# Thirty-two experts: one counted loop, or the loop written out; and where GpSimd stores y

## The reference, cut to what matters

```python
# 2048 tokens, D = 1024, 32 experts, FF = 256, two experts a token
eid, weights = route(h)                        # 4096 assignments
xb = h_pad[buf_tok].reshape(n_blocks, 128, d)  # tokens sorted by expert, padded to 128
def expert_block(xblk, e):
    return (silu(xblk @ w_gate[e]) * (xblk @ w_up[e])) @ w_down[e]
out = zeros.at[buf_tok].add(yb * buf_w[:, None])
```

## Time and profile before

| what | value |
|---|---|
| median of 3 runs | 3301.76 us (3297.97 to 3304.68) |
| the profiled execution: own time / its span | 3296.91 / 3295.3 us |
| TensorE busy | 2678.3 us, 81% of the span |
| TensorE weight load / VectorE / ScalarE / GpSimd | 64% / 55% / 50% / 16% |
| row gathers L1266 | x194, busy 199.6 us |
| stores of y L1282 | x101, busy 121.0 us, idle before 338.3 us, 322.3 of it ended by ScalarE's y |
| splits L1330 / L1372 | x256 / x256, 1047 / 1221 ns |
| HBM traffic | 167 GB/s over the span |

### The profile page before, as it was taken

One profiled execution on the slowest core, in us unless ns is written; L12 is line 12 of the kernel. 1 busy time (PEld: TensorE's weight loads), 2 busy tenths in 40 slices (PEclk: granted clock), 3 DMA queues, 4 the chain that ended last, 5 costly groups with the idle time before them and its releaser, 6 DMA issues. The chain is left out here.

```text
span 3295.3 us, 49089 instructions
## 1 busy us (share of the span) xinstructions
PE 2678.3 (81%) x12246; PEld 2124.9 (64%) x12247; DVE 1821.4 (55%) x3423; ACT 1640.8 (50%) x2254; POOL 528.3 (16%) x792
## 2 busy tenths in 40 slices
PE   4999969999699678888883999999699488888840
PEld 3777747777588556666662777777588366666630
DVE  3444434444356546455554688877466576545645
ACT  3444544454344346455553566765344365545633
POOL 0000000000001134334330000000011244333410
PEclk8999979999899789999996999999799799999975
DMA  3111121111444279778866445431544399777857
GB/s 110 34 50 45 51 64 45 45 51 41 152 135 152 73 266 323 238 248 293 273 202 221 165 164 167 165 115 58 176 132 147 134 354 319 234 233 242 280 204 280
DMA packets 358062, 550.28 MB, mean 167 GB/s; under 512 B 32097, under 2 KB 273905, under 8 KB 353905
## 3 DMA queue, kind: packets, MB, share of 16 engines
q1 hardware_dynamic: 323296, 436.20, 40.6%
q0 software_dynamic: 32400, 104.95, 8.6%
q10 hardware_dynamic: 2304, 8.39, 0.6%
HBM read 428.29 MB, written 121.18 MB: 167 GB/s over the span
## 5 line engine op out<-in xcount | busy, mean ns | idle before, releaser
L1372 DVE TENSOR_TENSOR experts_gu_lo<-experts_gu_raw,experts_gu_hi (+1 forms) x256 | 296.7, 1221 | 151.3 <-ACT experts_gu_hi L1330 151.3
L117 PE MATMUL experts_ps<-experts_gu_hi,experts_hT_hi 128*128 (+1 forms) x760 | 321.5, 423 | 48.9 <-issue 25.6
L1330 ACT ACTIVATE experts_gu_hi<-experts_gu_raw (+1 forms) x256 | 249.8, 1047 | 121.6 <-DMA experts_gu_raw<-in_moe_w_up 76.9
L119 PE MATMUL experts_ps<-experts_gu_hi,experts_hT_lo 128*128 (+1 forms) x760 | 304.3, 400 | 0.0
L118 PE MATMUL experts_ps<-experts_gu_lo,experts_hT_hi 128*128 (+1 forms) x760 | 304.0, 400 | 0.0
L117 PE MATMUL route_ps<-route_w_hi,route_src_hi 128*128 128x512 f32 x512 | 213.2, 416 | 59.6 <-DVE route_w_lo L958 59.6
L887 POOL MEMSET route_empty<- 128x512 int32 x2 | 1.1, 549 | 1439.2 <-POOLq L159 1439.2
L1266 POOL DMA_INDIRECT experts_rows<-h_rows,experts_source_now x194 | 199.6, 1029 | 171.9 <-POOL experts_source_now L1262 138.8
L1384 DVE TENSOR_TENSOR experts_hT_lo<-experts_ps,experts_hT_hi 128x512 fp32r<-128x512 f32 x194 | 133.2, 687 | 156.3 <-ACT experts_hT_hi L1308 151.8
L1423 PE MATMUL experts_ps<-ident,experts_rows 128*128 128x128 f32 x776 | 122.1, 282 | 117.0 <-DMA experts_rows<-h_rows,experts_source_now 116.6
L117 PE MATMUL gla_ps<-gla_wvg_hi,gla_hT_hi 128*128 128x512 f32 x512 | 212.7, 415 | 0.0
(11 more groups left out here) (304 smaller groups left out, 6511.2 us busy)
## 6 DMA issues: line engine op xcount, KB each, us to landing
experts_gu_raw<-in_moe_w_gate SPq DMA_DIRECT2D x64, 1024.0 KB
experts_gu_raw<-in_moe_w_up SPq DMA_DIRECT2D x64, 1024.0 KB, 12.5
experts_wd_raw<-in_moe_w_down SPq DMA_DIRECT2D x64, 1024.0 KB, 6.0
gla_w_raw<-in_gla_w_in SPq DMA_DIRECT2D x18, 1024.0 KB, 6.6
route_src<-oT_rows SPq DMA_DIRECT2D x32, 512.0 KB, 4.2
x_rows<-route_x_new SPq DMA_DIRECT2D x32, 512.0 KB, 2.9
h_rows<-route_h SPq DMA_DIRECT2D x64, 256.0 KB, 2.3
lru_y_ab<-y_rows SPq DMA_DIRECT2D x16, 1024.0 KB, 7.7
```

The lines of the kernel that those rows point to most:

```text
L117: nc.tensor.matmul(out, w_hi, x_hi, start=first, stop=False)
L119: return nc.tensor.matmul(out, w_lo, x_hi, start=False, stop=last)
L1330: nc.scalar.activation(gu_hi[:, slot(e), of_part(c)], gu_raw[:, slot(e), of_part(c)], ACT.Copy)\
L1372: nc.vector.tensor_tensor(gu_lo[:, slot(e), of_part(c)], gu_raw[:, slot(e), of_part(c)], gu_hi[:, slot(e), of_part(c)].bitcast(F32), ALU.s ...
```

## The change

**The loop over experts is written out 32 times** on ScalarE, VectorE, TensorE, GpSimd and SyncE. The route stage packs four counts into one word, in base 32 (`PACK`, `place_value`), with one multiply and one reduce in place of a scan and its two neighbours. Each engine reads eight words into registers once, before its first expert, takes a count out of a word by shift and mask, and keeps the running sum in a register. The slots of gate/up become constants, so the `stand` before those splits goes; TensorE's `down` keeps its register address.

**GpSimd's order**: in iteration g it gathers the first half for block g+1, stores the y of g-1 (not of g), then gathers the second half. The list of a block is kept one place later (`LAG` 4).

**The start of the stage**: two memsets (`wd_hi`, `wd_lo`) go from GpSimd to VectorE, and the first column of `sources` is made on its own, so that the first gather waits for that alone.

```diff
+PACK, PACK_BASE = 4, 32
...
-            step(nc.vector.tensor_tensor_scan(upto[:], k.ones_row[:], nblk[:], 0.0, ALU.mult, ALU.add))
-            step(nc.vector.tensor_tensor(upto[:], upto[:], nblk[:], ALU.subtract))
-            step.add(nc.vector.tensor_copy(k.blocks[:], nblk[:]))
-            step.add(nc.vector.tensor_copy(k.block_at[:], upto[:]))
-            step.wait()
+            by_word = nblk[:].rearrange("p (w i) -> p w i", i=PACK)
+            step(nc.vector.tensor_tensor(by_word, by_word,
+                                         k.place_value[:].unsqueeze(1).to_broadcast([P, E // PACK, PACK]),
+                                         ALU.mult))
+            step(nc.vector.tensor_reduce(packed[:], by_word, AX.X, ALU.add))
+            step(nc.vector.tensor_copy(k.blocks[:], packed[:]))
...
+        def expert_blocks(eng, each, before=None):
+
+            words = [eng.value_load(k.blocks[0:1, w:w + 1], min_val=0, max_val=PACK_BASE ** PACK - 1)
+                     for w in range(E // PACK)]
+            first = 0
+            for e in range(E):
+                n = (words[e // PACK] // PACK_BASE ** (e % PACK)) % PACK_BASE
                 if before:
-                    before(e, s)
+                    before(e, first)
                 with eng.Fori(0, n) as b:
-                    (each or each_of(n))(e, b, nc.s_assert_within(s + b, min_val=0, max_val=MAX_BLOCKS - 1))
...
+                    each(e, b, nc.s_assert_within(first + b, min_val=0, max_val=MAX_BLOCKS - 1), n)
+                first = nc.snap(first + n)
...
         def slot(e):
-            return slice(e % 2, e % 2 + 1) if isinstance(e, int) else bass.ds(e % 2, 1)
+            return slice(e % 2, e % 2 + 1)
...
-            with sp.Fori(0, E - 2) as e:
+            for e in range(E - 2):
...
+            def each(e, b, g, n):
+                last = 1 - (n - b + (SLOTS - 2)) // SLOTS
+                column = (e * SLOTS + b + 1 + last * (SLOTS - 1 - b)) % (E * SLOTS)
+                column = nc.s_assert_within(column, min_val=0, max_val=E * SLOTS - 1)
+                name_rows(0, column, g + 1)
+                gather(0, g + 1)
+                name_targets(g - 1)
+                store_y(g - 1)
+                name_rows(1, column, g + 1)
+                gather(1, g + 1)
+                keep_list(column, g + 1)
...
+            nc.vector.memset(wd_hi[:, 1].bitcast(F32), 0.0)
+            nc.vector.memset(wd_lo[:, 1].bitcast(F32), 0.0).then_inc(wd_zeroed, 1)
```

More of the change, by code:

```diff
@@ L209, in _ @@
             done.add(pool.memset(k.eps[:], EPS))
+            for i in range(PACK):
+                done.add(pool.memset(k.place_value[:, i:i + 1], float(PACK_BASE ** i)))
             done.add(pool.iota(k.token[:], [[2 * P, NT], [1, 2]], base=0, channel_multiplier=2))
@@ L1219, in load @@
             def load(e, landed, into, w):
-                if not (isinstance(e, int) and e == 0):
+                if e:
                     sp.wait_ge(landed, nth_dma(e - 1))
-                sp.dma_start(into, w[bass.ds(e, 1)].rearrange("e (k p) c -> p e k c", p=P)).then_inc(landed, DMA)
+                sp.dma_start(into, w[e:e + 1].rearrange("e (k p) c -> p e k c", p=P)).then_inc(landed, DMA)
             def load_gu(e):
@@ L1328, in split_gu @@
                 for c in range(PARTS):
-                    stand(act)
                     nc.scalar.activation(gu_hi[:, slot(e), of_part(c)], gu_raw[:, slot(e), of_part(c)], ACT.Copy)\
@@ L1347, in before, with each @@
             def before(e, first):
-                if not is_last(e):
+                if e + 1 < E:
                     split_gu(e + 1)
                 split_wd(e, first)
-            def each(e, b, g):
+            def each(e, b, g, n):
                 take_aT(g)
@@ L1445, in _ @@
             pe.wait_ge(zeroed, 1)
+            pe.wait_ge(wd_zeroed, 1)
             for b in range(2):
```

101 lines of the change are left out of this document (45 added, 56 removed).

## The result

The changed kernel takes **3214.71 us** at the median of 4 runs (3209.87 to 3217.18), against 3300.60 for the kernel before (4 runs, 3297.97 to 3304.68): a ratio of 0.9737, 95% interval 0.972 to 0.9754. That is 86 us less, where the forecast of 3178 us meant about 123. The profiled execution took 3209.87 us, with a span of 3208.1 us.

A forecast was written before the change was run, and what follows sets the result against it. TensorE's waits in both experts stages bound it: 77.6 + 74.9 us idle and 13 of clock, 165.5 at stake. Less 30 (transfers), 14 (store chain), 2.5 (aT), plus 1 (starts): 120 us gained, 3178 us for the median; range 3148 to 3238.

The forecast's parts named there:

- Reads at the turn: Two register reads with checks go from TensorE's 62 turns between experts, worth up to 49.9 us of its waits.
- The rest of the aT chain: Earlier ScalarE splits remove nearly all 31.1 us of down products' waits for aT's low part; 2.5 us charged as left.
- GpSimd's order: the first gather: Issued ahead of the store, 3.4 us into the block, it lands before its transposes; worth up to 69.9 us of row waits.
- The second gather: On GpSimd, it takes the first gather's old place in time and is due 3.4 us later, leaving 1.5 us to spare.
- The clock: Most of 13 us lost to TensorE's half clock in both experts stages returns, since row waits cause it.
- The store chain: Store, landing, y, store: charged 14 us (0 to 47). As a rival it paces every block: 3211 us, chance 0.15.
- The full stretches: In 255 us where transfers pace the experts stages, 30 us of TensorE's 40 us idle stays; bounds 10 and 40.
- More instructions: The written-out loop adds about 26 instruction pieces for TensorE and 30 for the rest; counted 0 us.
- Rows stay late: Rival: the second gather takes over the first's wait and clock dips stay; 61 us gained, 3236 us, chance 0.15.
- Late instructions: Rival: engines stand until the 56 added instruction pieces are fetched in the experts stages; 3357 us, chance 0.03.
- refetched loops: Rival: repeated inner loops straddling two instruction pieces are fetched again, 52 fetches; 3344 us, chance 0.03.
- no difference: Rival: the turn's reads and gathers lie beside transfers that bound both experts stages; chance 0.02.

The follow-up runs named there:

- e4: The changed kernel, but each engine loads the packed word again at every expert instead of eight words once before the loop: 3223.9 us.
- e1: The experts' loop written out with packed counts as in the changed kernel, but GpSimd's order and lag 3 of the kernel before: 3252.6 us.
- f1: The changed kernel, but from the third expert on each weight load brings only an eighth of its bytes: 3098.4 us.
- e6: The changed kernel with the copy of the target row numbers made by ScalarE instead of GpSimd: 3210.3 us.
- e3: The changed kernel with both gathers ahead of the preceding block's store on GpSimd: 3299.2 us.
- e2: The kernel before with GpSimd's new order alone (lag 4), keeping the loop over experts and its register loads: 3263.7 us.
- e5: The changed kernel with TensorE's transposes of the second half of the rows moved behind the down products: 3407.0 us.
- f2: The changed kernel with ScalarE's and VectorE's copies of aT moved ahead of the next expert's weight splits: 3237.3 us.

## Why the prediction was right, and where it was off

The range (3148 to 3238) holds the time, the direction was right, and both mechanisms acted. The likeliest case was 37 us too fast.

- **Reads at the turn, up to 49.9 us.** Right, and too small. All 49.9 us of idle are gone, and 60 turns gave back 0.24 us each of overlap that the idle column doesn't hold: 15 us. e4 narrows it down: a single read at each turn costs little (2.2 us of waits). Which of the second read, the loop's branches and the register addresses cost most stays open.
- **The rest of the aT chain, 2.5 us.** Wrong as told. That ScalarE's splits start at once behind its last rows is so (the splits of 1230.17 follow the rows of 1229.66 without a gap), and e1, which has only that part, is left with 4.1 us of aT_lo waits. With the new order 25.7 us are back, in few and long ones (13, up to 6.3 us, against 31 of at most 1.5). Blocks then run at TensorE's pace into the runs of one-block experts, and the weights come late, ahead of each of the 13 (2.54 us at 1244.15). f1, whose splits are the same, has none of these waits, so the transfers and not the splits are the cause. In the sum this belonged to the full stretches.
- **GpSimd's order: the first gather.** Right in the main: it is released by the transposes, and of its 69.7 us of waits 6.4 are left. It is issued 4.3 us into the block (median), not 3.4.
- **The second gather, "1.5 us to spare, a thin cover".** This is the step that failed. It took the second gather to be issued at the place in a block that the first had before, and so to keep 1.5 us. The first had been issued 9.0 us after a block's first gate/up product (median over both windows); the second is now issued at 10.4. What the same edit puts between the two gathers on GpSimd's queue (the rest of one issue, a copy, a store, a copy, and two waits of 0.9 us for its own copies) makes 5.6 us at the median, and that uses up the 1.5: a slow landing is then a wait. The step moved was costed for the store and for y, not for the gather right behind it. 40.1 us of row waits stayed, 33.6 of them the second gather's, where the sum had none outside the full stretches. e6 and e3 point to the queue, f1 shows that it takes the loaded landing with it.
- **The clock, 13 us back.** None came back. The waits left are fewer (55 against 145) but as long, up to 3 us for rows, and the lower level follows them. By the windows' means, 1% of 510 and 3% of 492 us are 20 us, where the same reckoning gave 5.6 + 10.6 = 16 before (the prediction took 13). So some 4 us more were lost than before.
- **The store chain, 14 us (bounds 0 and 47).** Named directly, TensorE waits for y 3.9 us in all. The chain acts on another path than the one priced: a y that waits for its store makes the next store late, and with it the second gather. Its share of the 40.1 us of row waits was not told apart from the queue's. Where the store is issued 2 us later (e3), it holds the down products and costs more than the rival's 47 us (84 us in all).
- **The full stretches, 30 us left (10 to 40).** f1 says that all of what is left, 71.9 us of idle but for 7, goes away when the weight loads are small. The 30 was too low, and the waits it leaves out are those of the two points above on aT and the second gather.
- **More instructions, 0.** Right: 28 and 38 more packets, no stall of TensorE. The Trainium skill's rule ("Runtime: NRT & Kernel Launch", section "Instruction fetch mechanics", a taken branch out of a window of two pages stalls) would have cost 88 us by the estimate given; the trace shows none of it. The same section names such stalls as one reason why kernels prefer full unrolling. Writing the loop out did gain 47.6 us here (e1), but the loop before had fetched next to nothing in its stage (3 packets), so the gain was not in the fetches.
- **Not foreseen.** The stages ahead of the first experts stage have the same code and yet took 5.8 us more (it begins at 1156.1 and not 1150.3 us); in every kernel with the loop written out it begins at 1152.7 to 1158.7, in e2 at 1149.2. Against the kernel before, the delay comes in steps of up to 1.6 us. Three of them (1.0 to 1.6 us) fall on stretches of 3.4 us at half clock, from 254, 681 and 1009 us, that the kernel before does not have. Why they come was not found. What is left of the difference, 5 us where 1 was forecast, lies between the windows and around them, mostly at the stages' starts.

Set against the forecast of 120: 25 us less idle gone, 17 of the clock (13 not gained, 4 more lost), 6 in the stages ahead; 15 of overlap and 4 at the starts more. That makes 91, against 87 between the two profiled executions; the means of the clock are rounded to 1%, which is worth more than the 4 us left. That the range held is no proof of its parts: the turns gave more than was forecast and the rows and the clock less, and these errors partly cancel.

**The rivals.** "Rows stay late" described the mechanism (the second gather takes over the wait of the first, the clock dips stay) but kept nearly all 70 us of it; 30 went. The store chain gave the nearest time, 3211, though it does not pace the blocks: it only helps to make the second gather late. The truth lies between the forecast and the late rows. Late instructions, refetched loops and no difference are out.

## What to carry to other kernels

When a transfer's issue is moved ahead in an engine's queue, price the issue next behind it as well, with every copy, semaphore and issue that now stands between: more than half of the row waits stayed because the second gather came 1.5 us later than the first had, beside loaded transfers. Before moving work on one engine, follow the in-order queues of all that take its result; e5 and f2 each removed the wait they aimed at and made a longer one two engines on. A wait can cost more than the idle time shown for it: here 0.24 us of broken overlap each, and behind the long ones the clock.

## What the runs showed of the hardware

- GpSimd waits 0.83 to 0.91 us between its own 0.20 us copy and the indirect transfer that takes the copied index, wherever it waits for nothing else (175 times in the changed kernel's trace).
- The same issue of a gather on GpSimd takes 1.0 us, and 2.34 while VectorE splits weights (1337.42, VectorE's 2.29 us split running). In the changed kernel's trace the 96 gathers whose issue met no split took 0.99 us on average and 1.03 at most; the 98 that met one took 1.71, and 2.14 where it was mostly the split of the down weights. Before, 57 met a split, none of them that of the down weights. The mean over all gathers rose from 1.03 to 1.35 us, over the first halves alone to 1.52. No run kept gathers and splits apart, so what that would give back is open.
- The clock's loss follows the length of waits, not their sum alone: with 114.4 us of idle in 126 waits e2 was granted 1.00 and 0.99, with 110.0 us in 59 longer ones e1 0.97 and 0.96, and with 192.3 us in 62 waits e5 0.90 and 0.89.
